# Handing out the gate projection as 2,2,2,2 contraction steps in a group's last step

## The reference

```python
def hybrid_layer(x, g, w_in, w_out, lq1, lk1, lq2, lk2, subln_g, rpb, lam_init):
    h = rms_norm(x, g)
    z = jnp.einsum('bsd,de->bse', h, w_in)
    qd, kd, vd, qn, kn, vn, gate = jnp.split(z, cuts, axis=-1)
    ...
    o_da = diff_attention(qd, kd, vd, lam, lam_init, subln_g)
    ...
    o_na = neighbourhood_attention(qn, kn, vn, rpb)
    o = jnp.concatenate([o_da, o_na], axis=-1) * jax.nn.silu(gate)
    return x + jnp.einsum('bse,ed->bsd', o, w_out)
```

## Time and profile before

| | |
|---|---|
| median of 3 runs | 1637.2 us |
| the profiled execution | 1635.22 us, of which the span 1632.5 us |
| PE busy | 1526.5 us, 94% of the span, 8800 matmuls |
| DVE busy | 1040.4 us (64%) |
| ACT busy | 710.2 us (44%) |
| POOL busy | 414.9 us (25%) |
| granted PE clock, 72 to 665 us (layer 1's groups) | 1.00 |

### The profile page before, as it was taken

How to read it: one execution, slowest core, us unless ns; L and a number is a source line. 1 busy time by engine, 2 the same in 40 slices (tenths; PEclk the granted TensorE clock), 3 DMA queues, 4 the chain that set the end, 5 groups by cost and what they waited for, 6 DMA issues and landing times. The chain is left out here.

```text
span 1632.5 us, 27307 instructions
## 1 busy us (share of the span) xinstructions
PE 1526.5 (94%) x8800; PEld 1259.8 (77%) x8800; DVE 1040.4 (64%) x2185; ACT 710.2 (44%) x1408; POOL 414.9 (25%) x414
## 2 busy tenths in 40 slices
PE   3999999999999999889979999999999999997995
PEld 2778787877888888678767878787878888886874
DVE  6377777777666666763145777878776666667422
ACT  4245554545444444432224454545453434345231
POOL 4222222223211112101542222232332020200152
PEclk9999999999999999989989999999999999998997
DMA  8100111011101020301101100101111111112013
GB/s 229 55 27 20 33 31 32 32 56 33 56 33 55 28 59 26 129 9 44 40 27 52 33 21 29 35 26 39 49 40 49 39 48 39 48 48 95 27 52 129
DMA packets 39262, 79.65 MB, mean 49 GB/s; under 512 B 18832, under 2 KB 18832, under 8 KB 39184
## 3 DMA queue, kind: packets, MB, share of 16 engines
q1 hardware_dynamic: 39184, 78.67, 15.2%
HBM read 67.12 MB, written 15.47 MB: 51 GB/s over the span
## 5 line engine op out<-in xcount | busy, mean ns | idle before, releaser
L734 PE MATMUL proj<-h_hi,w_hi 128*128 128x512 f32 x1248 | 531.3, 426 | 31.0 <-DVE h_lo L1147 11.0
L736 PE MATMUL proj<-h_hi,w_lo 128*128 128x512 f32 x1248 | 494.1, 396 | 0.0
L735 PE MATMUL proj<-h_lo,w_hi 128*128 128x512 f32 x1248 | 491.5, 394 | 0.0
L475 POOL TENSOR_TENSOR w_lo<-w_raw,w_hi 128x1024 fp32r<-128x1024 f32 x84 | 201.3, 2396 | 673.4 <-ACT w_hi L584 661.5
L734 PEld LDWEIGHTS proj<-h_hi,w_hi 128*128 128x128 f32 x1248 | 236.9, 190 | 109.4 <-issue 36.0
L736 PEld LDWEIGHTS proj<-h_hi,w_lo 128*128 128x128 f32 x1248 | 236.5, 190 | 54.8
L735 PEld LDWEIGHTS proj<-h_lo,w_hi 128*128 128x128 f32 x1248 | 238.2, 191 | 37.0
L1077 DVE TENSOR_TENSOR pt_lo<-turn,pt_hi 128x512 fp32r<-128x512 f32 x192 | 132.2, 688 | 153.7 <-ACT pt_hi L610 153.7
L610 ACT ACTIVATE pt_hi<-turn 128x512 fp32r<-128x512 f32 x192 | 114.9, 599 | 217.9 <-PE turn L827 217.8
L1069 DVE CUSTOM_DVE_ANT_0 prob<-scores,dist 128x1024 f32<-128x1024 f32 x128 | 156.0, 1219 | 9.8 <-PE scores L770 9.2
L634 ACT ACTIVATE prob<-prob,nm,escale_now 128x1024 f32<-128x1024 f32 x128 | 158.1, 1235 | 2.2 <-DVE nm L1073 2.2
(11 more groups left out here) (125 smaller groups left out, 2369.1 us busy)
## 6 DMA issues: line engine op xcount, KB each, us to landing
w_raw<-chunks SPq DMA_DIRECT2D x84, 512.0 KB, 3.4
mixed_dram<-gate SPq DMA_DIRECT2D x28, 256.0 KB, 2.1
edge<-bias_dram SPq DMA_DIRECT2D x32, 224.0 KB, 3.7
h_lo<-mixed_dram SPq DMA_DIRECT2D x14, 512.0 KB, 6.6
xt<-x_t SPq DMA_DIRECT2D x8, 512.0 KB, 7.5
out_t<-prob SPq DMA_DIRECT2D x8, 512.0 KB, 3.6
bias_dram<-bias_rows SPq DMA_DIRECT2D x16, 240.0 KB, 6.0
gate<-lam_vecs SPq DMA_DIRECT2D x1, 256.0 KB, 9.4
```

What stands on the lines that cost most here:

```text
L475: pool.tensor_tensor(w_lo[:, b], w_raw[:], f32(w_hi[:, b]), ALU.subtract).then_inc(w_lo_done, 1)
L734: pe.matmul(dst, a_hi, b_hi, start=start, stop=False)
L735: pe.matmul(dst, a_hi, b_lo, start=False, stop=False)
L736: return pe.matmul(dst, a_lo, b_hi, start=False, stop=stop)
```

## The change

In a last step that has a group behind it, the parts become 0-1, 2-3, 4-5 and 6-7. The fourth part, empty before, is given out directly after the mix, ahead of the two V transposes (before, the call stood behind them and issued nothing).

```diff
                     parts = [range(0, 2), range(2, 5), range(5, 8)]
                     if last_step:
-                        parts = [range(0, 2), range(2, 5), range(5, 8), ()]
+                        parts = [range(0, 2), range(2, 4), range(4, 6), range(6, 8)]
...
                     weigh(g, t - 1)
                     if last_step:
+                        fill(3)
                         turn_v(behind, 0)
                         turn_v(behind, 1)
-                        fill(3)
                         score(behind, 1)
```

## The result

The changed kernel takes 1644.1 us (median of 8 runs, 1641.35 to 1645.9) beside 1636.77 for the kernel before in the same series (8 runs, 1634.74 to 1640.09): a ratio of 1.0042 with a 95% interval of 1.003 to 1.0054, so 0.3 to 0.5% slower. The forecast was 1642.1 us and +4.9; measured were +6.9 by the ratio (the two medians differ by 7.3). The profiled execution of the changed kernel took 1643.67 us, its span is 1641.9 (before: 1632.5).

The account below looks back on a forecast made before the run. PE was taken as the bound (busy 94% of the span), its order with waits being the time; 6 x 0.11 + 2 x 0.2 + 6 x 0.63 = 4.9 us on 1637.2 gave 1642.1 us, range 1638.8 to 1645.8.

Parts of the forecast that it names:

- DA to DA: Six last steps of DA groups before another DA group: 0.80 us gap filled, V transposes end later, +0.11 us each.
- change-over from the mix: On PE, from the last mix product to the moved projection run: taken as 0.1 us.
- DA to NA: Two last steps of DA groups before an NA group: V transposes end later, mostly covered, +0.2 us each.
- the step failed that took the V copy to start 0.2 us later: ACT's V copy in the two DA to NA steps: start moves from 416.25 to about 416.44, cost +0.2 us.
- NA to NA: Six last steps of NA groups before another NA group: no gap ahead of the V transposes to fill, +0.63 us each.
- The shift of the px chain with `turn_p` 1: NA to NA steps: the ACT and DVE chain behind `turn_p` 1 starts 0.69 us earlier and ends at 494.04.
- the wait for px_lo: NA to NA steps: PE ready for the mix at 493.45 waits 0.6 us; the mix starts 0.74 us earlier.
- the unchanged 0.76 us behind the V transposes: NA to NA steps: the idle gap ahead of the last `turn_u` moves along and keeps its 0.76 us.
- The rival without a difference: NA to NA steps: chain to px_lo shorter than charged or change-over nil, 0.25 us each; 1639.6 us; chance 0.17.
- 0.79 us for the six moved matmuls: Estimate from the Trainium skill's 131 ns per matmul; with it the sum would shrink to about 3 us.
- The faster one: DA groups: first low part in time, no wait at `turn_p` 1, 6 x 0.80 us gained; 1633.6 us; chance 0.06.
- The much slower one: NA steps: px chain hangs on ACT's exponentials, mix does not move, 1.58 us each; 1647.8 us; chance 0.07.

Follow-up runs that it names:

- Run 1: Against the kernel before: parts 2,2,2,2 only in the last steps of DA groups, NA last steps as before; 1638.15 us, 0.9993.
- Run 3: Against the kernel before: NA last steps 2,2,3,1, one contraction step behind the mix taken from ahead of `turn_p` 1; DA unchanged; 1638.75 us, 1.0.
- Run 4: Against the kernel before: NA last steps 2,3,2,1, one contraction step behind the mix taken from behind `turn_p` 1; DA unchanged; 1643.69 us, 1.0033.
- run 8: Changed kernel plus five unused 256-column products between `turn_u` and the mix in NA last steps; 1642.51 us, 1.0027 of the kernel before.
- run 10: Changed kernel plus five unused 256-column products ahead of the mix in NA last steps, measured again; 1642.18 us, 1.0027 of the kernel before.
- run 2: Against the kernel before: parts 2,2,2,2 only in the last steps of NA groups, DA as before; 1643.08 us, 1.0038.
- run 9: The changed kernel itself measured once more, nothing altered; 1643.4 us, 1.0039 of the kernel before.
- run 11: NA last steps 2,2,2,2, fourth part behind the V transposes, DA as before, plus five unused products ahead of the mix; 1634.82 us, 0.9974 of the kernel before.
- run 7: Against the kernel before: NA last steps 2,2,2,2 with the fourth part behind the V transposes, DA as before; 1638.76 us, 1.0003.

## Why the prediction was right, and where it was off

The direction, the range and the place were right: slower, by waits that the two taken contraction steps leave ahead of the mix.

*DA to DA*, forecast +0.11 us a step. Measured 83.65 against 83.69 us per period, -0.04. The mechanism was as told. The forecast had `turn_v` 0 start 0.16 us later (248.18 and 248.02), and it started 0.04 earlier. Of these 0.20 us, 0.13 are the mix: its last product came 247.81 - 165.67 = 82.14 us behind the V transposes of the group ahead, before 247.00 - 164.33 = 82.67, so 0.53 earlier and not 0.40. The change-over from the mix was 0.06 and not 0.1, and the run behind it took 249.32 - 247.87 = 1.45 us instead of 1.48.

*DA to NA*, forecast +0.2 us, measured -0.1 (from the V transposes of the previous group to the last `turn_u`: 86.57 and 86.59 us after, 86.70 both times before). Here the step failed that took the V copy to start 0.2 us later and counted this as a delay of all that follows. Counted from the V transposes of the group ahead, ACT's first V copy started at 417.48 - 332.86 = 84.62 us, before 416.25 - 331.65 = 84.60. And before, `turn_u` had waited for POOL, longer than for V; POOL's chain hangs on the mix, and its end (417.59 + 0.61 = 418.20 before, 418.05 + 0.61 = 418.66 after) moved with it from 418.20 - 331.65 = 86.55 to 418.66 - 332.86 = 85.80, so `turn_u` now goes by the V copies. Run 1 bounds both DA terms together at nothing measurable.

*NA to NA*, forecast +0.63 us, measured 82.86 against 82.16, +0.70. The shift of the px chain with `turn_p` 1, the wait for px_lo and the unchanged 0.76 us behind the V transposes were as told; the change-over was 0.17 (582.00, the last mix product, to 582.17) instead of 0.1. Runs 3 and 4 confirm the reason given: what is taken from behind `turn_p` 1 is lost, what is taken from ahead of it is given back.

*What the sum lacked* is the clock. The undisturbed terms add up to 6 x 0.70 - 6 x 0.04 - 2 x 0.1 = 3.8 us. The changed kernel with the waits filled (runs 8 and 10) takes 0.27% more than before, 4.4 us. The rest up to 0.42%, about 2.5 us, fits the falls, though the intervals of the two ratios overlap: in the three profiled executions with these NA steps (the changed kernel, runs 2 and 9) 5 of 18 steps fell, at 1.44 us, so 6 x 5/18 x 1.44 = 2.4 us per execution on average. The profiled execution of the changed kernel closes as well: 3.8 + 3 x 1.44 = 8.1 us against the 8.0 that are left of the two spans' 9.4 without the first group's 1.4. The forecast also said that PE's busy time would stay within a microsecond or two, and it rose by 11.4. In the forecast the idle time ahead of the mix was priced by its own length alone. The forecast of 4.9 came nearer to the result than its reasons deserved, as the DA terms were too large by 1.5 us and the missing one was larger than that: two errors that partly cancel.

*Two sums.* The rival without a difference comes to 1637.2 + 2.6 = 1639.8 us and not 1639.6. With 0.79 us for the six moved matmuls, the same steps give about 6 x 0.24 = 1.4 us (the NA steps; nothing in the DA ones) and not 3. Neither bears on the forecast; the six took 1.44 to 1.49 us.

*The rivals.* The one without a difference needed an NA price of 0.25; it was 0.70. The faster one needed the first low part before PE's arrival at `turn_p` 1; PE waited there, as the row had said. The much slower one needed a px chain that does not follow `turn_p` 1; it followed (2.71 us from `turn_p` 1 to the mix, before 494.83 - 492.07 = 2.76).

## What to carry to other kernels

Filler work between two waits has a side: taken from ahead of the instruction that starts the dependent chain it comes back in full, taken from between that instruction and its reader it becomes idle time. Moved work belongs where PE is idle now: behind the V transposes it filled a gap and gained 0.3%, ahead of them the same step gained nothing. And an idle gap, here one ahead of small matmuls, can cost more than its length, so compare the durations of one instruction over all executions of its loop before counting gaps.

## What the runs showed of the hardware

- Where PE had waited about 0.6 us and then run 2.5 us of small products, the granted clock dropped to its lower level in a third of the steps (12 of 36), at about 1.5 us each; with the same wait filled by unused products this was never seen in eighteen steps (runs 8, 10 and 11). Without that wait a drop was seen in the last steps only behind the 1.45 us for POOL (2 of 16).
- In the straight-line DA to NA steps the last `turn_u` is followed by the next projection after 0.4 us (419.45 to 419.86 after); the same 0.4 stands where a loop of NA groups ends (664.54 to 664.99 before), and 0.7 where it turns (500.24 to 500.94). When the V copies are done before PE comes to `turn_u`, as in run 7, both shrink, to 0.08 at the end of the loop (1462.14 to 1462.22) and 0.12 at its turn.
